# A decoder layer with PEER experts on one core: u and v loaded in pairs of blocks, act in rows of 5.6 KB, SyncE's loops written out, another order of loads at the change of stage

## The reference, cut to what matters

```python
def block(xb):                       # 128 tokens at a time
    ...                              # top-k by product keys -> idx, sc
    gate = jax.nn.softmax(sc.astype(jnp.float32), axis=-1)
    act = jax.nn.gelu(jnp.einsum('thed,td->the', u_table[idx], xb).astype(jnp.float32), approximate=False)
    return jnp.einsum('the,thed->td', (gate * act).astype(xb.dtype), v_table[idx])
x = x + peer(h, peer_w_q[l], peer_keys_1[l], peer_keys_2[l], peer_u[l], peer_v[l])
```

## Time and profile before

| what | before |
|---|---|
| runs, median (lowest to highest) | 1458.32 us (1455.82 to 1459.24), 3 runs |
| the profiled execution, its time | 1460.59 us |
| its span in the trace | 1458.8 us |
| mean granted clock of PE | 0.995 |
| PE busy | 1427.0 us, 98% of the span |
| PEld (weight loads) | 1367.2 us, 94% |
| DVE | 1186.6 us, 81% |
| POOL | 765.1 us, 52% |
| ACT | 636.7 us, 44% |
| DMA | 423.15 MB, mean 290 GB/s |

### The profile page before, as it was taken

How to read it: one execution, slowest core, us unless ns; L and a number is a source line. 1 busy time by engine, 2 the same in 40 slices (tenths; PEclk the granted TensorE clock), 3 DMA queues, 4 the chain that set the end, 5 groups by cost and what they waited for, 6 DMA issues and landing times.

```text
span 1458.8 us, 24697 instructions
## 1 busy us (share of the span) xinstructions
PE 1427.0 (98%) x8813; PEld 1367.2 (94%) x8813; DVE 1186.6 (81%) x2337; ACT 636.7 (44%) x1035; POOL 765.1 (52%) x428
## 2 busy tenths in 40 slices
PE   7999889999999999999999999899999999999998
PEld 6879678888999999999999999799999999999998
DVE  5747563388989999989999997588898998998994
ACT  4463472222433333447777775332243343433332
POOL 2524171233677678865545554256566665566630
PEclk9999999999999999999999999999999999999999
DMA  7400211312579989999999999989999999999991
GB/s 270 152 30 1 115 35 43 112 62 73 165 259 343 327 299 364 404 377 341 372 357 358 355 403 390 376 292 411 410 412 409 410 410 410 410 411 410 410 357 58
DMA packets 165902, 423.15 MB, mean 290 GB/s; under 512 B 13348, under 2 KB 85924, under 8 KB 163912
## 3 DMA queue, kind: packets, MB, share of 16 engines
q1 hardware_dynamic: 119624, 254.48, 46.8%
q0 software_dynamic: 46208, 167.81, 30.2%
HBM read 376.00 MB, written 46.20 MB: 289 GB/s over the span
## 4 chain that ended last, share of the span: by engine, by line
PE 90%; DMA 5%; DVE 2%; issue 1%; ACT 1%; SPq 0%; DVEq 0%; ACTq 0%
PE banks L2048 32%; PE banks L1812 16%; PE banks L2119 10%; PE banks L2121 10%; PE banks L2120 10%; PE banks L2087 5%; DMA act_in<-act_scratch 3%; DMA u_raw<-in_uT 2%; PE banks L2027 1%; PE banks L1842 1%; PE banks L1886 1%; PE banks L1944 1%; DVE x_res L1631 1%; PE banks L1964 1%; PE banks L1963 1%
## 5 line engine op out<-in xcount | busy, mean ns | idle before, releaser
L818 POOL DMA_INDIRECT rows<-in_v,idx x160 | 283.3, 1771 | 192.9 <-DVE x_res L1631 130.7
L2119 PE MATMUL banks<-w_hi,v_hi 128*128 128x352 f32 x1024 | 330.0, 322 | 1.9 <-DVE w_lo L1730 1.9
L2120 PE MATMUL banks<-w_lo,v_hi 128*128 128x352 f32 x1024 | 329.3, 322 | 0.0
L2121 PE MATMUL banks<-w_hi,v_lo 128*128 128x352 f32 x1024 | 329.3, 322 | 0.0
L1157 ACT ACTIVATE v_hi<-v_raw 128x1024 fp32r<-128x1024 f32 x128 | 134.4, 1059 | 287.4 <-DMA v_raw<-in_v 277.8
L818 POOL DMA_INDIRECT rows<-in_u,idx x160 | 191.1, 1195 | 124.7 <-DVE z L1613 91.1
L794 POOL TENSOR_TENSOR u_lo<-u_raw,u_hi 128x1024 fp32r<-128x1024 f32 x66 | 163.9, 2487 | 95.1 <-ACT u_hi L1052 47.9
L2048 PE MATMUL banks<-h_hi,u_hi 128*128 128x352 f32 x1024 | 191.3, 329 | 6.9 <-ACT act_kept L1078 6.9
L2048 PE MATMUL banks<-h_lo,u_hi 128*128 128x352 f32 x1024 | 198.0, 328 | 0.0
L2119 PEld LDWEIGHTS banks<-w_hi,v_hi 128*128 128x128 f32 x1024 | 192.3, 188 | 2.8 <-issue 2.6
L2120 PEld LDWEIGHTS banks<-w_lo,v_hi 128*128 128x128 f32 x1024 | 192.3, 188 | 0.0
(11 more groups left out here) (284 smaller groups left out, 2084.0 us busy)
## 6 DMA issues: line engine op xcount, KB each, us to landing
u_raw<-in_uT SPq DMA_DIRECT2D x128, 512.0 KB
v_raw<-in_v SPq DMA_DIRECT2D x128, 512.0 KB
gate_scratch<-stage SPq DMA_DIRECT2D x11, 2048.0 KB
gate_pairs<-gate_scratch SPq DMA_DIRECT2D x15, 1408.0 KB, 18.4
act_scratch<-act_out SPq DMA_DIRECT2D x116, 176.0 KB
act_in<-act_scratch SPq DMA_DIRECT2D x29, 704.0 KB
wi_raw<-in_w_in SPq DMA_DIRECT2D x8, 1024.0 KB, 6.9
wq_raw<-in_w_q SPq DMA_DIRECT2D x8, 1024.0 KB, 5.5
```

What stands on the lines that cost most here:

```text
L818: nc.gpsimd.indirect_dma_start(ROW_KB[U_SLOT[s]][:], None, a["u"] if kind in "ab" else v_flat, bass.IndirectOffsetOnAxis(ap=at_x, axis=0)) ...
L2119: mm(y, v_hi[x][:, ds], w_hi[q][:, j, :], start=start, stop=False)
L2120: mm(y, v_hi[x][:, ds], w_lo[q][:, j, :], start=False, stop=False)
L2121: return mm(y, v_lo[x][:, ds], w_hi[q][:, j, :], start=False, stop=stop)
```

## The change

Five things, in the order of the diff:
- v: `v_raw` becomes four pairs of buffers, and SP loads two blocks with one transfer of 1 MB in which each partition's row is 8 KB (`load_v(pair, m)`), from `v_pairs`, a second copy of v that the host lays out pair by pair; the gathers still read the old layout. One semaphore for each pair; the load of a pair waits for PE to be done with the second of the two blocks that were there. The places (`V_KB`) are in another order.
- u: the host lays `uT` out in pairs, SP loads two blocks at once (8 KB a partition) in the turn of every odd block, where the second of the two was issued before. The first pair no longer starts with u(0) ahead of the wait for the last query but one.
- act: `act_scratch` is [32 groups, 128, 4, 352] instead of [128 blocks, 128, 352]. A save still writes 1408 bytes a partition; the load of a group reads 5632 bytes a partition in one piece.
- SP's loops over the trips of PRE and MAIN are written out (the loop of the second product stays).
- the order at the change of stage: in the last trip save_gates(5, 0) is issued after the turn of block 119 (with the pair 122, 123 ahead of it) and not in that of block 117. Then come the pair 124, 125 (after u_lo(121)), v 0 and 1 (after block 119 is done with, no longer after the gates are saved), the pair 126, 127 (after u_lo(123)), the waits for the saved act and gates, `gates`, v 2 and 3, `load_pair`, v 4 and 5, and, after the last block, v 6 and 7.

The instructions of PE, SCALAR, VECTOR and POOL and their order are the same. The diff, cut to its core:

```diff
@@ -349,8 +349,9 @@
...
-        V_KB = (38, 42, 46, 50, 62, 66, 54, 58)
-        v_raw = [at(f"v_raw{x}", kb, [P, D]) for x, kb in enumerate(V_KB)]
+        V_KB = (62, 66, 38, 42, 46, 50, 54, 58)
+        v_pairs = [at(f"v_pairs{m}", kb, [P, 2, D]) for m, kb in enumerate(V_KB[::2])]
+        v_raw = [v_pairs[x // 2][:, x % 2, :] for x in range(V_RING)]
         v_lo = [at(f"v_lo{x}", kb, [P, D], F32R) for x, kb in enumerate(V_KB)]
...
@@ -365,7 +366,7 @@
...
-        act_d = nc.dram_tensor("act_scratch", [E_BLOCKS, P, NA], F32).ap()
+        act_d = nc.dram_tensor("act_scratch", [GROUPS, P, GROUP, NA], F32).ap()
         h2x_d = nc.dram_tensor("h2x_scratch", [NE, D], F32).ap()
...
@@ -435,7 +436,7 @@
...
         triT_done = sem("triT_done")
-        u_in = [sem(f"u_in{i}") for i in range(4)]
+        u_in = [sem(f"u_in{m}") for m in range(2)]
         uhi_ready = sem("uhi_ready")
...
@@ -449,7 +450,7 @@
...
         gate_saved = [sem(f"gate_saved{i}") for i in range(2)]
-        v_in = [sem(f"v_in{x}") for x in range(V_RING)]
+        v_in = [sem(f"v_in{m}") for m in range(V_RING // 2)]
         actg_in = [sem(f"actg_in{i}") for i in range(2)]
...
@@ -576,30 +577,30 @@
...
-            def load_u(n, j):
-                sp.dma_start(u_raw[:, j % 4, :, :],
-                             a["uT"][bass.ds(n, 1)].rearrange("o p k e -> (o p) k e")).then_inc(u_in[j % 4], 16)
+            def load_u(pair, m):
+                sp.dma_start(u_raw[:, 2 * m:2 * m + 2, :, :].rearrange("p n k e -> p (n k e)"),
+                             a["uT"][bass.ds(pair, 1)].rearrange("o p n k e -> (o p) (n k e)")).then_inc(u_in[m], 16)
...
             sp.wait_ge(wqlo_ready, PH)
-            load_u(0, 0)
             arrived(sp, ("qry", PH - 2, 1))
-            for j in range(1, 4):
-                load_u(j, j)
-
-            def save_act(n, j):
+            for m in range(2):
+                load_u(m, m)
+
+            def save_act(n, j, g):
                 sp.wait_ge(act_ready, n + 1)
-                sp.dma_start(act_d[bass.ds(n, 1)].rearrange("o p t -> (o p) t"),
+                sp.dma_start(act_d[bass.ds(g, 1), :, j % GROUP, :].rearrange("o p t -> (o p) t"),
                              act_out[:, j % RING, :]).then_inc(act_saved[j % RING], 16)
...
                     wait_ulo(sp, i, j, PRE_BODY)
-                    load_u(n + 4, j)
+                    if j % 2:
+                        load_u(i * (PRE_BODY // 2) + (j + 3) // 2, j // 2)
                     if not (isinstance(n, int) and n < 2):
-                        save_act(n - 2, j + 2)
+                        save_act(n - 2, j + 2, i * (PRE_BODY // GROUP) + (j - 2) // GROUP)
...
@@ -609,7 +610,7 @@
...
                         sp.dma_start(h2x[x * NE:(x + 1) * NE, :], h2x_d).then_inc(h2x_in, 16)
-            with sp.Fori(SHARE_FROM // PRE_BODY, PRE_TRIPS) as i:
+            for i in range(SHARE_FROM // PRE_BODY, PRE_TRIPS):
                 pre(i)
...
@@ -618,14 +619,15 @@
...
-            def main(i):
+            def main(i, last=False):
                 for j in range(MAIN_BODY):
...
                     wait_ulo(sp, i, PRE + j, MAIN_BODY)
-                    load_u(n + 4, j)
+                    if j % 2:
+                        load_u(i * (MAIN_BODY // 2) + (PRE + j + 3) // 2, j % 4 // 2)
                     if not isinstance(n, int) or n - 2 < SAVED:
-                        save_act(n - 2, j + 2)
-                    if j == MAIN_BODY // 2 + 1:
+                        save_act(n - 2, j + 2, i * (MAIN_BODY // GROUP) + (PRE + j - 2) // GROUP)
+                    if j == MAIN_BODY // 2 + 1 and not last:
                         save_gates(i, 0)
...
@@ -634,16 +636,16 @@
...
             main(0)
-            with sp.Fori(1, MAIN_TRIPS - 1) as i:
+            for i in range(1, MAIN_TRIPS - 1):
                 main(i)
-            main(MAIN_TRIPS - 1)
-
-            def load_v(n, x):
-                sp.dma_start(v_raw[x][:], a["v"][bass.ds(n, 1)].rearrange("o p d -> (o p) d")
-                             ).then_inc(v_in[x], 16)
+            main(MAIN_TRIPS - 1, last=True)
+
+            def load_v(pair, m):
+                sp.dma_start(v_pairs[m][:].rearrange("p n d -> p (n d)"),
+                             a["v_pairs"][bass.ds(pair, 1)].rearrange("o p n d -> (o p) (n d)")).then_inc(v_in[m], 16)
             def load_act(g, q):
-                sp.dma_start(act_in[q][:], act_d[bass.ds(g * GROUP, GROUP)].rearrange("n p t -> p n t")
+                sp.dma_start(act_in[q][:], act_d[bass.ds(g, 1)].rearrange("o p n t -> (o p) n t")
                              ).then_inc(actg_in[q], 16)
...
@@ -657,26 +659,26 @@
...
                 wait_ulo(sp, 0, n, 1)
-                load_u(n + 4, n % 4)
-
+                wait_ulo(sp, 0, n + 1, 1)
+                load_u((n + 4) // 2, n % 4 // 2)
+
+            save_gates(MAIN_TRIPS - 1, 0)
             post_load_u(POST)
-            post_load_u(POST + 1)
-            sp.wait_ge(gate_saved[0], 16 * (CHUNKS + 1) // 2)
-            for b in range(2):
-                load_v(SAVED + b, b)
+
+            sp.wait_ge(z_done, POST)
+            load_v(SAVED // 2, 0)
             post_load_u(POST + 2)
-            for b in range(2, 4):
-                load_v(SAVED + b, b)
             for q in range(RING):
...
             sp.wait_ge(gate_saved[1], 16 * (CHUNKS // 2))
+            sp.wait_ge(gate_saved[0], 16 * (CHUNKS + 1) // 2)
             sp.dma_start(gates[:].rearrange("p c n t -> p c (n t)"), half_pair(SAVED // PAIR, 1)).then_inc(gates_in, 16)
-            post_load_u(POST + 3)
+            load_v(SAVED // 2 + 1, 1)
             load_pair(NK // PAIR - 1, 0)
-            for b in range(4, V_RING):
-
-                sp.wait_ge(z_done, (POST, POST, E_BLOCKS - 1, E_BLOCKS)[b - 4])
-                load_v(SAVED + b, b)
+            load_v(SAVED // 2 + 2, 2)
+
+            sp.wait_ge(z_done, E_BLOCKS)
+            load_v(SAVED // 2 + 3, 3)
...
@@ -691,14 +693,15 @@
...
                                      half_pair(SAVED // PAIR, 0)).then_inc(pairs_in[m], 16)
-                for j in range(GROUP):
+                for j in range(0, GROUP, 2):
                     b = p * GROUP + (j + V_RING)
...
-                    sp.wait_ge(v_done, p * GROUP + (j + 1))
-                    n = SAVED + b if isinstance(p, int) and b < E_BLOCKS - SAVED else b - (E_BLOCKS - SAVED)
-                    load_v(n, r % 2 * GROUP + j)
+                    sp.wait_ge(v_done, p * GROUP + (j + 2))
+                    n = p * 2 + (j + V_RING) // 2
+                    n = n + SAVED // 2 if isinstance(p, int) and b < E_BLOCKS - SAVED else n + (SAVED - E_BLOCKS) // 2
+                    load_v(n, r % 2 * 2 + j // 2)
...
@@ -1041,7 +1044,7 @@
...
-                act.wait_ge(u_in[j], n // 4 * 16 + 16 if isinstance(n, int) else (n - j) * 4 + 16)
+                act.wait_ge(u_in[j % 4 // 2], n // 4 * 16 + 16 if isinstance(n, int) else (n - j) * 4 + 16)
...
@@ -1153,8 +1156,8 @@
...
-                act.wait_ge(v_in[x], turn * 16 + 16)
-                nc.scalar.activation(v_hi[x][:], v_raw[x][:], ACT.Copy).then_inc(vhi_ready, 1)
+                act.wait_ge(v_in[x // 2], turn * 16 + 16)
+                nc.scalar.activation(v_hi[x][:], v_raw[x], ACT.Copy).then_inc(vhi_ready, 1)
...
@@ -1700,7 +1703,7 @@
...
                 x = b % V_RING
-                nc.vector.tensor_tensor(v_lo[x][:], v_raw[x][:], v_hi[x][:].bitcast(F32), ALU.subtract
+                nc.vector.tensor_tensor(v_lo[x][:], v_raw[x], v_hi[x][:].bitcast(F32), ALU.subtract
                                         ).then_inc(vlo_ready, 1)
...
@@ -2212,9 +2215,10 @@
...
-        "uT": np.asarray(peer_u)[0].reshape(NK, NK, KD, P).transpose(0, 3, 2, 1),
+        "uT": np.asarray(peer_u)[0].reshape(NK // 2, 2, NK, KD, P).transpose(0, 4, 1, 3, 2),
         "u": np.asarray(peer_u)[0],
         "v": np.asarray(peer_v)[0].reshape(NK, NK, D),
+        "v_pairs": np.asarray(peer_v)[0].reshape(NK // 2, 2, NK, D).transpose(0, 2, 1, 3),
     }
...
```

## The result

The changed kernel is slower: median 1476.5 us (1472.46 to 1486.03, 4 runs) against 1458.13 (1455.82 to 1459.24); ratio 1.0128, interval 1.0098 to 1.0158. The profiled execution took 1478.15 us, its span is 1476.4, before 1460.59 and 1458.8: 17.6 us more.

A forecast was written before the change was run, and what follows sets the result against it. PE, idle only 8.8 of 1076 us, was taken as the bound. Handover -1.6 and second product -1.9 gave -3.5, taking the profiled 1460.59 to 1457.1; the median, 2.3 below that execution, gave 1454.8 us, range 1446 to 1464.

The forecast's parts named there:

- First product: Blocks 0 to 119: loading u in pairs delays even blocks but not PE; cost 0, up to 1 us.
- The handover: Change from u to v stage: the new load order starts the second product 1.6 us earlier; bounds -9.5 to +2.2.
- no wait before block 120: Handover: u blocks 122 and 123 load ahead of the last gate save, so PE's first wait goes, -2.19 us.
- a wait inside block 125 for v 2 and 3: Handover: v 2 and 3, moved behind the gates, make PE wait 3.9 us; block 125 still ends 2.0 ahead.
- block 122, forecast 1.2 (0 to 2.2): Handover: block 122 could start at 924.6 but starts at 925.9, a 1.2 us wait, leaving PE 1.0 ahead.
- 125 landed by 924.3: Handover: at 2.38 us a block after 919.58, u block 125 landed by 924.3; bytes ahead of its end unchanged.
- Second product: The v stage: 8 KB v rows, helped by act's fewer rows, remove both w_lo waits, -1.9 us; bounds -1.9 to +6.
- The rival of the pace: V stage: the clock holds and matmuls stay near 167 ns, adding 23.6 us, 1478 in all; chance 0.14.
- The rival of the clock: Handover: PE's clock falls again in the 3.9 us wait, 1.0 worse than before, total 1457.4; chance 0.14.
- pairs of 8 KB rows in the v stage lose to the gathers: V stage: engines share by bytes, so 8 KB rows win no time against gathers; about +6 us, 1463; chance 0.09.

The follow-up runs named there:

- e1: The changed kernel with u loaded in single blocks again, all else as changed; median 1451.31 us, ratio 0.9954 to the kernel before.
- e5: The kernel before with u loaded in pairs and SP's loops written out; median 1488.35 us, ratio 1.0184.
- e7: The changed kernel with each u pair still issued in the odd block's turn, but as two transfers with a semaphore each; median 1466.11 us, ratio 1.0043.
- e9: The changed kernel with the gate saves of the first five main-stage trips cut to a sixteenth, output not the layer's; median 1451.14 us, ratio 0.9955.
- e11: The kernel before, unchanged, run and traced a second time; median 1457.14 us, ratio 0.9987.
- e6: The changed kernel with u in single blocks and SP's old order at the change of stage; median 1454.94 us, ratio 0.9967.
- e3: The kernel before with v loaded in pairs and nothing else; median 1457.36 us, ratio 0.9995.
- e4: The kernel before with the new act layout and SP's loops written out; median 1455.71 us, ratio 0.9981.
- e10: The changed kernel with u single, first v-row gathers held until the last u block is rounded, v 2 and 3 ahead of the gates; 1447.57 us, ratio 0.9927.
- e12: The changed kernel with u and v single, first v-row gathers held until the last u is rounded, v 2 and 3 before gates; 1444.44 us, ratio 0.9905.

## Why the prediction was wrong, step by step

The forecast was 1454.8 us, 3.5 less than before; measured are 1476.5, 18.4 more.

- **First product, "Cost 0, up to 1 us": wrong, 18.** This is the step that failed. The step took block 71, in a stage without saves, as the place "where u arrives latest", and waved the even blocks behind a save through with "their time is not on PE's path before either". That holds for the kernel before, by the earlier trace rows, and says nothing of the changed one. The working was at hand: a pair is issued a turn later (799.10 for 787.87 in the trace), stands behind the save all the same, and its even block lands with the odd one. The kernel before shows what such a u has to spare only where it is at its least, and the earlier trace rows showed none at all for block 122, for which SCALAR waited 7.13. The slack of an even block behind one save of the main stage was not read. The cost is five waits for act_out, 13.1 us together, the longest 4.3. e1, e5, e7 and e9 settle it. (In the first stage too the place was not the worst: SCALAR waited 5.54 for u(58), and the 2.0 lost there start from it.)
- The clock was then charged only at the change of stage. After the waits of 3.32 and 4.29 it cost (1 - 0.50) x 5.3 = 2.7 and (1 - 0.72) x 5.2 = 1.5 us in the main stage. With the 13.1 of waiting that is 17.3; 1.3 came back as faster pace in between, and 16.0 is the loss.
- **The handover, -1.6: wrong in its path; measured +2.7, of which 1.6 is the main stage's last wait (above).** Right: no wait before block 120, and a wait inside block 125 for v 2 and 3 (forecast 3.9, measured 3.82 in the changed kernel and 4.25 in e1). Wrong: block 122, forecast 1.2 (0 to 2.2), measured 4.89. The pair 124, 125 was issued at 930.6 behind the 2 MB and was rounded at 945.75; that "125 landed by 924.3" in the old order didn't carry over to one in which the save begins later. In e1, with single blocks, it is 4.19 too, so this part is the order's, not the pairs'. The clock didn't hold. And the two stretches of the +2.7 were entered at different paces: the second trace of the kernel before (e11), entered at 158 ns like the changed kernel's, took 61.9, so at like pace the changed kernel's 60.0 is 1.9 less. That this is close to the -1.6 is luck, since the waits it was added up from came out otherwise. That the new order still wins 3.8 (e1 against e6) comes from less waiting in all, 9.0 us and not 12.3.
- **Second product, -1.9: right in size (-2.7), wrong in its cause.** The forecast gave it to v's rows of 8 KB and let act's rows help. e3 and e4 show the reverse: act's rows alone bring it, v's pairs alone don't (and e5 has the written-out loops that e4 also has, with 495.8).
- **Rivals.** The rival of the pace gave 1478 and the profiled execution took 1478.15; that is chance. The v stage ran at 159 ns in this and in all other traces. The rival of the clock was right in that the clock fell. That pairs of 8 KB rows in the v stage lose to the gathers was wrong: no wait for w_lo in the changed kernel.

## What to carry to other kernels

A transfer made larger lands whole: its first half is as late as its last, and later by the turn that it was held back. Before two loads are joined, look at each place where they stand behind something large in their queue, and ask what the first of the two has to spare there; a wait that the old kernel doesn't have shows only as slack. And where an effect of some us is to be timed, compare the stretches of traces at the same pace, not the medians alone.

## What was not expected of the hardware

**PE's matmuls have two paces at one granted clock.** 128x352 matmuls came every 158 or every 167 ns, at full clock both, and stayed so for hundreds of matmuls. What changed it was small. In e3 (timeline of PE, start and length of each group):

```profile
427.97 1.43 PE L2049 MATMUL banks<-h_hi,u_lo 128*128 128x352 f32 x8
429.79 1.56 PE L2049 MATMUL banks<-h_hi,u_hi 128*128 128x352 f32 x8 [0.39 <-issue]
431.19 1.49 PE L2049 MATMUL banks<-h_lo,u_hi 128*128 128x352 f32 x8
```

Eight matmuls took 1.27 us up to an idle time of 0.39, ahead of block 16, and 167 ns each after it, up to block 66: 285.3 us for the first stage and not 274.7. In the changed kernel the group at 588.15 (above) began 0.16 late, since SCALAR had waited 5.5 us for u(58); after it the pace was 167 to 623, which is most of the 2.0 us lost in the first stage. Idle times of 0.28 in e9 and 0.43 in e5, within 4 us of the same place, changed nothing, so a gap is an occasion and no rule. It went back to 158 at the nine transposes near 624 and in some cases where the clock had been halved; but behind a halved clock it also went from 158 to 167 (e4 at block 121, e11 at block 126). In the v stage it was 158 to 160 in every trace. What decides it stays open.

It would explain why the runs of one kernel scatter: the ten runs of e10 lie at 1441.7 to 1445.4 (five) and 1449.8 to 1454.5 (five), and the whole main stage differs by 8.2 us from one pace to the other. The profiled ones fit: e10's, at 1441.95, ran the main stage at 158 ns, and e12's, at 1449.96, at 167. Only one execution of each kernel was traced (two of the kernel before), so that the pace splits the ten isn't shown, and it isn't all: block 0 starts between 367.1 and 371.9 us in the thirteen traces.
